# Three in-place slots for the split weights instead of two, loops written out, and banded values projected by features and then transposed

## The reference, cut to what matters

```python
def hybrid_layer(x, ...):                       # block 1, twice
    h = rmsnorm(x, norm_g)
    proj = h @ w_in                             # split into a, b, c, d: four groups of 256 features
    y_a = conformer_conv(a_u, a_v, ...) * silu(a_z)
    y_b = short_gated_conv(b_b, b_c, b_x, conv_b_w) * silu(b_z)
    y_c = window_gqa(c_q, c_k, c_v, swa_sink) * silu(c_z)      # banded attention, window 128
    y_d = neighborhood_attn(d_q, d_k, d_v, na_rpb) * silu(d_z)
    return x + concat(y_a, y_b, y_c, y_d) @ w_out

for l in range(2):                              # block 2, twice
    h = rms_norm(x, g_mix); proj = h @ w_in     # u_pool, q_lat, kv_lat, u_lru, gate_logit (3 x 1024)
    y_pool, y_mla, y_lru = pool_mixer(...) @ w_pool_proj, mla(...) @ w_mla_o, rg_lru(...) @ w_lru_proj
    merged = sigmoid(gates) . (y_pool, y_mla, y_lru)           # summed over the three branches
    x = x + merged @ w_out
    x = x + square(relu(rms_norm(x) @ w_ff1)) @ w_ff2          # 1024 -> 4096 -> 1024
```

## Time and profile before

| | |
|---|---|
| median of 3 runs | 2136.82 us (2133.42 to 2136.87) |
| profiled execution: its time / its span | 2136.14 us / 2133.9 us |
| PE busy | 1984.1 us, 93% of the span |
| PEld, DVE, ACT, POOL busy | 77%, 55%, 35%, 49% |
| mean granted TensorE clock | 0.968 |
| traffic | 175.22 MB read from HBM, 83 GB/s over the span |

### The profile page before, as it was taken

One profiled execution on the slowest core, in us unless ns is written; L12 is line 12 of the kernel. 1 busy time (PEld: TensorE's weight loads), 2 busy tenths in 40 slices (PEclk: granted clock), 3 DMA queues, 4 the chain that ended last, 5 costly groups with the idle time before them and its releaser, 6 DMA issues.

```text
span 2133.9 us, 27204 instructions
## 1 busy us (share of the span) xinstructions
PE 1984.1 (93%) x9276; PEld 1640.6 (77%) x9276; DVE 1169.0 (55%) x2121; ACT 745.3 (35%) x1091; POOL 1054.7 (49%) x1301
## 2 busy tenths in 40 slices
PE   6889799789788999799999999999997999999997
PEld 5678678678677888687878888778886878888886
DVE  7885657876576555745433232765557454233225
ACT  3333434334422554423313223335444333132231
POOL 5434246334253444555655555644445655555553
PEclk9899999899899999899999999999998999999998
DMA  4112122121121122222222232221222222222221
GB/s 165 66 66 70 59 73 99 52 70 61 47 101 60 60 80 80 85 92 96 82 104 99 89 106 79 99 80 62 77 83 95 79 99 92 101 86 96 98 98 59
DMA packets 28030, 178.58 MB, mean 84 GB/s; under 512 B 3872, under 2 KB 4000, under 8 KB 7456
## 3 DMA queue, kind: packets, MB, share of 16 engines
q1 hardware_dynamic: 24192, 169.88, 22.8%
q10 hardware_dynamic: 3744, 7.45, 1.0%
HBM read 175.22 MB, written 2.10 MB: 83 GB/s over the span
## 4 chain that ended last, share of the span: by engine, by line
issue 42%; POOL 34%; PE 22%; DVE 1%; POOLq 0%; ACT 0%; DVEq 0%; ACTq 0%
POOL W_lo L445 34%; PE bank L459 22%; DVE X L1926 0%; POOLq L440 0%; PE bank L512 0%; PE bank L505 0%; POOLq L442 0%; POOL SPARES L436 0%; DVE L L2186 0%; ACT MRG_hi L1017 0%; DVE MRG_lo L1464 0%; DVE PRE L2228 0%; DVE TMP L1487 0%; DVE PRE L2196 0%; ACT PR L1368 0%
## 5 line engine op out<-in xcount | busy, mean ns | idle before, releaser
L445 POOL TENSOR_TENSOR W_lo<-W_raw,W_hi 128x256 fp32r<-128x256 f32 x1280 | 1052.8, 858 | 1047.5 <-ACT W_hi L1012 1047.5
L459 PE MATMUL bank<-H_hi,W_hi 128*128 128x512 f32 x1272 | 509.3, 400 | 20.1 <-POOL W_lo L445 17.5
L459 PE MATMUL bank<-H_hi,W_lo 128*128 128x512 f32 x1272 | 500.1, 393 | 0.0
L459 PE MATMUL bank<-H_lo,W_hi 128*128 128x512 f32 x1272 | 499.9, 393 | 0.0
L1012 ACT ACTIVATE W_hi<-W_raw 128x2048 fp32r<-128x2048 f32 x160 | 305.4, 1909 | 333.7 <-PE bank L459 301.5
L459 PE MATMUL bank<-Y_hi,W_hi 128*128 128x512 f32 x956 | 382.5, 400 | 17.6 <-ACT PR L1368 10.0
L459 PE MATMUL bank<-Y_lo,W_hi 128*128 128x512 f32 x956 | 377.3, 395 | 0.0
L459 PE MATMUL bank<-Y_hi,W_lo 128*128 128x512 f32 x956 | 376.8, 394 | 0.0
L459 PEld LDWEIGHTS bank<-H_hi,W_hi 128*128 128x128 f32 x1272 | 242.1, 190 | 76.2 <-POOL W_lo L445 21.7
L459 PEld LDWEIGHTS bank<-H_hi,W_lo 128*128 128x128 f32 x1272 | 241.6, 190 | 52.1
L459 PEld LDWEIGHTS bank<-H_lo,W_hi 128*128 128x128 f32 x1272 | 242.3, 191 | 47.7
(11 more groups left out here) (300 smaller groups left out, 2403.5 us busy)
## 6 DMA issues: line engine op xcount, KB each, us to landing
W_raw<-in_stream SPq DMA_DIRECT2D x160, 1024.0 KB, 4.9
BT<-in_bias ACTq DMA_DIRECT2D x8, 320.0 KB, 3.1
X<-in_x ACTq DMA_DIRECT2D x4, 512.0 KB, 9.9
out<-X SPq DMA_DIRECT2D x8, 256.0 KB, 2.2
BT<-in_rope ACTq DMA_DIRECT2D x2, 512.0 KB, 3.5
MC<-in_causal ACTq DMA_DIRECT2D x2, 256.0 KB, 3.6
MS<-in_window ACTq DMA_DIRECT2D x1, 321.0 KB, 10.9
NM<-in_columns ACTq DMA_DIRECT2D x1, 320.0 KB, 11.2
```

The lines of the kernel that those rows point to most:

```text
L445: ins = nc.gpsimd.tensor_tensor(W[1][:, s, part], W_raw[:, s, part], W[0][:, s, part].bitcast(F32), ALU.subtract)
L459: mm = pe.matmul(out, lhs[a], rhs[b], start=(not begun and k == 0 and a == 0 and b == 0), stop=(not more and k == n - 1 and a == 1), skip_ ...
```

## The change

There are three slots (`SLOTS`), and `W_lo` now lies in the same memory as `W_raw`: the subtraction on POOL is in place. The memory stays the same, 3 x 2 x 8 KB for each partition in place of 2 x 3 x 8 KB. SP waits, before it issues unit n, for PE's end with unit n-3 (`consumed`). `prep` waits only for the landing and for ACT's own order; its place in ACT's list is the same. All hardware loops of PE, ACT, DVE and SP are written out with the spare instructions in them; POOL keeps one, over three units a turn. The values chunk `ck1` is projected like any other (features on the partitions), ACT copies it to `PRE[:, 1]`, PE turns it by four transposes into bank 5 after `scores(8)`, and ACT rounds that to `AV_hi`.

```diff
-    W_raw = sb("W_raw", [P, 2, 2048])
-    W = two("W", [P, 2, 2048])
+    W_hi = sb("W_hi", [P, SLOTS, 2048], F32R)
+    before = ExitStack()
+    with before:
+        W_raw = sb("W_raw", [P, SLOTS, 2048], F32, before)
+    W = (W_hi, sb("W_lo", [P, SLOTS, 2048], F32R))
...
     def _(sp):
-        with sp.Fori(0, UNITS // 2) as i:
-            for s in range(2):
-
-                sp.wait_ge(w_lo, 2 * i + s + 1)
-
-                sp.dma_start(W_raw[:, s, :], dram["stream"][bass.ds(2 * i + s, 1)].rearrange(
-                    "a p n -> p (a n)")).then_inc(w_raw[s], 16)
+        for n in range(UNITS):
+            if n >= SLOTS:
+                sp.wait_ge(*consumed(n - SLOTS))
+            sp.dma_start(raw_of(n % SLOTS), dram["stream"][n]).then_inc(w_raw[n % SLOTS], 16)
...
-                if name == "ck1":
-                    mm = token_major(pe, out, k % 2, c, tiles(NORMED))
-                elif name in ("o00", "o01"):
+                if name in ("o00", "o01"):
...
+            def banded_values():
+                pe.wait_ge(b1.vt.sem, b1.vt.at(l, "c"))
+                pe.wait_ge(b1.lo.sem, b1.lo.at(l, f"pt{STEPS - 1}a"))
+                for t in range(4):
+                    mm = pe.transpose(TB[1][:, t * P:(t + 1) * P], PRE[:, 1, t * P:(t + 1) * P], ident[:, :])
+                mm.then_inc(b1.vd.sem, 1)
...
                     scores(i)
+                    banded_values()
                     chunk("cz0")
...
-        def prep(b, l, k, after, step=0, back=0):
-
-            act.wait_ge(w_raw[k % 2], unit_fill(b, l, k) + 8 * step)
-            if after:
-                act.wait_ge(after[0].sem, after[0].at(*after[1:]) - back)
+        def prep(b, l, k):
+
+            n = unit(b, l, k)
+            act.wait_ge(w_raw[n % SLOTS], 16 * (n // SLOTS + 1))
             act.wait_ge(*own.last(1))
...
-                    hi(b1, l, "cv", AV[0][:, :, 0:P], bank_[:, :].rearrange("p (t n) -> p t n", t=4))
+                    act.wait_ge(b1.lo.sem, b1.lo.at(l, "cq1"))
+                    act.wait_ge(*own.last(1))
+                    nc.scalar.activation(PRE[:, 1, :], bank_[:, :], ACT.Copy) \
+                        .then_inc(b1.vt.sem, own.event(b1.vt, l, "c"))
...
-            with pe.Fori(0, 3) as f:
-                down(unit(2, l, 34) + 8 * f, "f", f, lambda count, n: count.at(l, "u0", "f", f) + (n - KT))
-                up(unit(2, l, 38) + 8 * f, "f", f,
+            for f in range(3):
+                down(34 + 8 * f, "f", f, lambda count, n: count.at(l, "u0", "f", f) + (n - KT))
+                up(38 + 8 * f, "f", f,
```

More of the change, by code:

```diff
@@ L421, in _ @@
+        for n in range(SLOTS):
+            sp.wait_ge(w_raw[n], 16 * len(range(n, UNITS, SLOTS)))
         for k in range(KT):
@@ L431, in _ @@
         n = 0
-        for first, times in [(w_lo, 2)] + [(c.sem, c.start) for c in COUNTS if c.start]:
+        for first, times in [(c.sem, c.start) for c in COUNTS if c.start]:
             for _ in range(times):
@@ L1094, in begin @@
                 k = n // 2 + 1
-                if k == 1:
-                    prep(1, l, 1, (b1.done, l, "av0"), back=1)
-                else:
-                    prep(1, l, k, (b1.done, l, B1_CHUNKS[2 * k - 3]))
+                prep(1, l, k)
             def chunk(name, begun=False):
@@ L1272, in _ @@
                     uk = 3 + 3 * jj
-                    if jj == 0:
-                        prep(2, l, uk + 1, (b2.done, l, "k00", "h", j), step=6 * j, back=1)
-                    else:
-                        prep(2, l, uk + 1, (b2.done, l, "g03", "h", j), step=6 * j)
+                    prep(2, l, uk + 1 + 6 * j)
                     def softmax(s):
@@ L1385, in merged @@
                        PRE[:, c, :], seg, i, scale=0.5)
-            with act.Fori(0, 3) as m:
-                own.enter(m, ACT_STEPS_M)
-                prep(2, l, 20, (b2.done, l, "t0", "m", m), step=2 * m, back=1)
-                prep(2, l, 21, (b2.br, l, "1", "m", m), step=2 * m)
+            for m in range(3):
+                prep(2, l, 20 + 2 * m)
+                prep(2, l, 21 + 2 * m)
                 merged("m", m, 2 * m)
                 gate_tanh(2 * m, "m", m, 22)
-                act.wait_ge(*own.last(1))
-                nc.scalar.activation(spare_a[:, :], ones[:, 0:1], ACT.Copy).then_inc(act_step, own.step())
-            own.leave(3)
-            prep(2, l, 26, (b2.done, l, "t1", "m", 2))
-            prep(2, l, 27, (b2.br, l, "1", "m3"))
+            prep(2, l, 26)
+            prep(2, l, 27)
             merged("m3", 0, 6)
@@ L1435, in _ @@
             nc.scalar.activation(spare_a[:, :], ones[:, 0:1], ACT.Copy).then_inc(act_step, own.step())
-            with act.Fori(0, 3) as f:
-                own.enter(f, ACT_STEPS_F)
-                down(36, 8 * f, "f", f)
-                up(39, 8 * f, "f", f, (b2.done, l, "d7", "f", f))
-                act.wait_ge(*own.last(1))
-                nc.scalar.activation(spare_a[:, :], ones[:, 0:1], ACT.Copy).then_inc(act_step, own.step())
-            own.leave(3)
+            for f in range(3):
+                down(36 + 8 * f)
+                up(39 + 8 * f, "f", f)
             for k in range(KT):
                 if k in (2, 4, 6) and l + 1 < DEPTH:
-                    prep(2, l, 60 + k // 2 - 1, (b2.done, l, f"d{k - 1}", "f3", 0))
+                    prep(2, l, 60 + k // 2 - 1)
                 elif k in (2, 4):
-                    prep(2, l, 60 + k // 2 - 1, (b2.done, l, f"d{k - 1}", "f3", 0))
+                    prep(2, l, 60 + k // 2 - 1)
                 if l + 1 < DEPTH:
@@ L2234, in merged @@
                     lo(b2, l, f"b{c}", at(1), PRE[:, c, :], at(0), seg, i, half=True)
-            with dve.Fori(0, 3) as m:
-                own.enter(m, DVE_STEPS_M)
+            for m in range(3):
                 merged("m", m, lambda c: b2.aux.at(l, f"t{c}", "m", m) - 2, 2 * m)
@@ L2240, in _ @@
                     third_gate("m", m, c)
-                dve.wait_ge(*own.last(1))
-                nc.vector.memset(spare_v[:, :], 0.0).then_inc(dve_step, own.step())
-            own.leave(3)
             merged("m3", 0, lambda c: b2.aux.at(l, f"t{c}", "m", 2), 6)
@@ L2279, in down @@
                     dve.wait_ge(b2.done.sem, b2.done.at(l, f"d{n}", seg, i))
-                    dve.wait_ge(*own.last(1))
+                    dve.wait_ge(*own.last(1 if n else 0))
                     scaled_ = PR[:, 1 if after else n % 2, :]
@@ L2300, in _ @@
                 layer_params(l + 1)
-            with dve.Fori(0, 3) as f:
-                own.enter(f, DVE_STEPS_F)
+            for f in range(3):
                 down("f", f)
                 up("f", f)
-                dve.wait_ge(*own.last(1))
-                nc.vector.memset(spare_v[:, :], 0.0).then_inc(dve_step, own.step())
-            own.leave(3)
             down("f3", 0, True)
```

222 lines of the change are left out of this document (120 added, 102 removed).

## The result

The changed kernel takes 2114.14 us, median of 4 runs (2113.04 to 2115.27), the one before 2136.24 (4 runs) on the same occasions: a ratio of 0.9899, 95% interval 0.9882 to 0.9916, so 21.6 us less (17.9 to 25.2); the medians differ by 22.1. The forecast was 2116.5 with a range of 2107 to 2129. The profiled execution took 2115.27 us, its span 2113.5. So the sum came out, but a loss that it had at nothing and gains that it had too small nearly cancelled.

What follows compares the result with a forecast made beforehand. Bounds: PE at its own rate in the feed-forward, over half the time, leaving single places with late weights or waits. Terms -8.0 - 3.9 - 5.1 - 1.6 - 1 = -19.6 from 2136.14 gave 2116.5 us, range 2107 to 2129.

Steps and rivals of the forecast that it cites:

- Banded values: Values chunk ck1 in block 1: fewer, longer matmuls plus transposes start cz0 4.0 us earlier a layer, -8.0 for two.
- Start of layer 1: Block 1: unit 20's earlier rounding no longer holds H_hi, removing DVE idle time; -3.9 us, at most -4.6.
- First merge gate: Block 2, both layers: unit 54's rounding no longer waits for PE; -2.6 and -2.5 us, together -5.1.
- End of the merge: Both layers: unit 61's rounding goes earlier, ending PE's wait through MRG_lo; -0.8 us each, -1.6 for two.
- In place: POOL's subtraction over its own input might be slower: 10% more gives 31 us, 2147 us; chance 0.07.
- Half clock: First merge gate: a shorter idle might let PE start at 2.4 GHz, 2.6 us more a layer, 2111; chance 0.09.
- rival 3: The half clock goes away at the merge gates: 2.6 us more won a layer, 2111 us; chance 0.09.
- Loops: Turns of the feed-forward and merge loops: writing them out wins 0.25 us a turn, taken as -1 (-0.4 to -3).
- Start: Kernel start: a third 1 MB transfer competes with X and the constants; taken as 0 (-0.5 to +2.5).
- Waiting for a DMA: Every unit: transfer, rounding and subtraction need 15.1 us at most against two units' 21.9, so waiting on PE costs nothing.
- rival 4: Half-gains: DVE pays for POOL's earlier work, start 2 us later, or raw slot released late; 2119 to 2125, chance 0.12.
- SBUF rule: Start of layer 1: two-input DVE instructions contend with GpSimd reading SBUF; priced at 0, or the term becomes -2.3.

Runs made afterwards that it cites:

- slots_only: The changed kernel with the banded values put back to token-major matmuls; three in-place slots and written-out loops stay: 2123.85 us, ratio 0.9951 to the kernel before.
- hold_72: The changed kernel with ACT's rounding of unit 72 held until DVE's parameter series has ended: 2112.78 us, ratio 0.9902 to the kernel before.
- params_spread: The changed kernel with all but two of DVE's 128x2 parameter operations moved into the following up projection: 2108.63 us, ratio 0.9879 to the kernel before.

## Why the prediction was right, and where it was not

*Banded values*, -4.0 a layer: 4.1 at `cz0`, by the steps named, wait for `AK_lo` included. Some 0.4 of it was given back behind it, and the part alone brought -7.7.

*Start of layer 1*, -3.9: 4.1 at `AK_lo`, and DVE's two idle times are gone. Right.

*First merge gate*, -2.6 and -2.5: the mechanism was right, the size too small: 4.2 at each gate (the table's 3.7 holds 0.5 lost ahead of the second). The term took the subtraction's durations as fixed, 8.26 and 7.77. They are not: one of its instructions takes 0.72 us alone and 1.18 beside a DVE operation of 512 columns with two inputs, and the units, moved ahead, had fewer of these beside them, 14.74 for both, 1.3 less. In three of the variants (`slots_only`, `hold_72`, `params_spread`) PE's first idle time there was 3.7 instead of 3.0, so 3.5 to 4.2 is the size.

*End of the merge*, -0.8: 0.8. *In place*: 6.50 against 6.51, so the slower side's mechanism is not there. *Half clock*: after idle times of 3.03 and 4.87 PE still started at the lower level, 0.79 and 0.80 us for the first matmul, so rival 3 did not happen at the merge gates. *Loops*, -1: 0.2 to 0.5 in each of six rounds, -2.6; undersized, since I took half of the turns as hidden behind `W_lo`. *Start*: 17.98 against 18.3; the 1.0 us lost by 184 comes later, at a wait for `PT_lo` that varies between executions. *Waiting for a DMA*: the roundings wait 192 us in all for their landing, and PE's rate in the feed-forward is unchanged.

What failed is the sentence that POOL's amount of work was unchanged and lay beside the same kind of DVE work before, so that it cost 0. At the start of layer 1, for which it was written, it held. But the sum took it for the whole kernel and has no term for the first down projection, where 4.5 us were lost, 3.7 of them in the series beside POOL; only rival 4 had such a loss, at a chance of 0.12. I had the SBUF rule in hand, took from it only that the two contend, and priced that by operations of 512 columns, 0.4 us more each, four of them. The price that matters is one for small operations: 0.5 us on top of 0.16, times the length of a dependent series. These 4.5 us were made up for by the merge gates (3.3 more than forecast), the loops (1.6 more) and waits that vary between executions. That the total came within 3 us is luck, not accuracy.

## What to carry to other kernels

Another slot pays at a few places where an instruction stands behind a wait that the slot removes; look for these in the list of the engine that did the waiting, and then move the work ahead, since its old place is now the limit. Work that starts earlier on GpSimd is not free even if GpSimd is idle half of the time: look what VectorE does in that very stretch, and count its small dependent operations and its operations with two inputs, each of which a running GpSimd instruction can hold up. The length of GpSimd's instructions is thus a setting of its own: long ones finish sooner and hold VectorE longer.

## What the runs showed of the hardware

A DVE operation of 128x2 numbers took 0.16 us alone and 0.38, 0.65 and 2.2 us beside POOL instructions of 128, 256 and 1024 columns. It held for TENSOR_TENSOR and for TENSOR_SCALAR on float32, the latter with one input; RECIPROCAL (0.17) and MEMSET (0.06) did not wait. A SCALAR_TENSOR_TENSOR of 128x512 took 0.75 us alone, 1.22 beside POOL instructions of 256 columns and 1.78 beside those of 512. POOL's subtraction of 2048 columns took 5.5 to 5.6 us in eight instructions with nothing but such a series on DVE, and about 4.8 in two. Writing over its own input cost POOL nothing (6.50 against 6.51). The level at which PE starts again did not follow the length of the idle time alone. In the kernel after it was 1.2 GHz after 3.03 us (0.79 us for the first matmul, at 860.77). At the start of block 2, after 3.92 us, it was 2.4 GHz for the first five matmuls, whose starts lie 0.23 to 0.33 us apart, and 1.2 GHz behind them, with starts 0.43 apart. PE's row there, then both stretches (length, PE busy, granted clock, DMA share, GB/s):

```profile
616.28 0.50 PE L511 MATMUL bank<-H_hi,W_hi 128*128 128x512 f32 x1 [3.92 <-POOL W_lo L461]
...
616.28:619.28 3.00, 3.00 (x9) 0.68 0.07 25
860.77:864.77 4.00, 4.00 (x9) 0.50 0.00 0
```

There the kernel before had started at 1.2 GHz after 4.37.
